# A two-layer hybrid decoder step: the S5 branch computed ahead of the retention's, sampled rows spread over more tiles, and the first tiles behind each norm multiplied before the inverse root is known

## What is computed

```python
u = rmsnorm(h, norm_g);  z = u @ w_in                 # one projection feeds three branches and three gates
s5_out  = glu(gelu(s5_scan(z_s5) + d*z_s5))           # complex diagonal state space, 32 groups of 16 channels
ret_out = silu(g) * groupnorm(retention(q, k, v))     # 4 heads, dk 128, dv 256
conv_out = silu(layernorm(depthwise_conv31(glu(z_conv))))
merged = sig(gate_s5)*(s5_out@s5_proj) + sig(gate_ret)*(ret_out@ret_proj) + sig(gate_conv)*(conv_out@conv_proj)
x = h + merged @ w_out
x = x + ffn(rmsnorm(x))     # layer 0: dense SwiGLU (2816); layer 1: top-2 of 8 experts (3584)
```

## Time and profile before

| | us |
|---|---|
| three runs | 1994.47, 2006.04, 2010.76; median 2006.04 |
| profiled execution | 2003.79 |
| its span (first to last instruction) | 2002.0 |

### The profile page before, as it was taken

One profiled execution on the slowest core, in us unless ns is written; L12 is line 12 of the kernel. 1 busy time (PEld: TensorE's weight loads), 2 busy tenths in 40 slices (PEclk: granted clock), 3 DMA queues, 4 the chain that ended last, 5 costly groups with the idle time before them and its releaser, 6 DMA issues.

```text
span 2002.0 us, 31584 instructions
## 1 busy us (share of the span) xinstructions
PE 1876.1 (94%) x11792; PEld 1591.1 (79%) x11792; DVE 1563.6 (78%) x1767; ACT 1198.4 (60%) x1277; POOL 364.9 (18%) x489
## 2 busy tenths in 40 slices
PE   7977799989998987999999999999999999999995
PEld 6866599979998976899877777777777777777774
DVE  6986697765545966877488888888888988889886
ACT  4343355444444452646476877777777776777775
POOL 7995109940000143000000000000000000000000
PEclk8998899989999997999799999999999999999998
DMA  5546754445555729455589999999999999999996
GB/s 186 171 121 164 148 174 153 165 148 181 179 179 157 212 84 244 110 173 169 220 332 353 382 364 369 373 364 382 355 369 367 373 380 356 370 363 378 381 352 237
DMA packets 98098, 527.54 MB, mean 264 GB/s; under 512 B 11863, under 2 KB 13431, under 8 KB 54359
## 3 DMA queue, kind: packets, MB, share of 16 engines
q1 hardware_dynamic: 86167, 488.69, 66.6%
q0 software_dynamic: 10784, 36.50, 8.0%
q10 hardware_dynamic: 1056, 1.08, 0.2%
HBM read 505.69 MB, written 20.54 MB: 263 GB/s over the span
## 4 chain that ended last, share of the span: by engine, by line
PE 76%; DVE 11%; issue 4%; DMA 4%; ACT 4%; POOL 0%; DVEq 0%; ACTq 0%; SPq 0%; POOLq 0%
PE bank L628 23%; PE bank L630 23%; PE bank L629 23%; DVE ring_parts L1423 2%; DMA out_ret_s<-zone 2%; DVE s5m_parts L1918 2%; DVE zone L1550 1%; PE bank L1000 1%; DMA zone<-in_sret 1%; PE bank L661 1%; ACT zone_parts L1364 1%; PE bank L954 1%; ACT ring_parts L1059 1%; DVE tmp L1614 1%; DVE zone L1446 0%
## 5 line engine op out<-in xcount | busy, mean ns | idle before, releaser
L1918 DVE TENSOR_TENSOR s5m_parts<-s5m,ring_parts 128x2048 fp32r<-128x2048 f32 x228 | 519.2, 2287 | 75.6 <-ACT ring_parts L1364 75.0
L1364 ACT ACTIVATE ring_parts<-s5m 128x2048 fp32r<-128x2048 f32 x228 | 431.7, 1917 | 87.0 <-DMA s5m<-in_experts 80.9
L1423 DVE TENSOR_TENSOR ring_parts<-ring,ring_parts 128x1024 fp32r<-128x1024 f32 x238 | 311.5, 1313 | 203.8 <-ACT ring_parts L1059 177.8
L628 PE MATMUL bank<-uT_parts,ring_parts 128*128 128x264 f32 x1312 | 388.4, 296 | 30.5 <-DVE uT_parts L1440 19.0
L629 PE MATMUL bank<-uT_hi,ring_parts 128*128 128x264 f32 x1312 | 382.4, 291 | 0.0
L630 PE MATMUL bank<-uT_hi,ring_parts 128*128 128x264 f32 x1312 | 381.2, 291 | 0.0
L628 PE MATMUL bank<-s5m_parts,work_parts 128*112 128x512 f32 x896 | 359.3, 401 | 1.1 <-DVE table_parts L1910 1.1
L1059 ACT ACTIVATE ring_parts<-ring 128x1024 fp32r<-128x1024 f32 x238 | 251.2, 1057 | 161.5 <-PE bank L630 125.7
L1918 DVE TENSOR_TENSOR s5m_parts<-s5m,zone_parts 128x2048 fp32r<-128x2048 f32 x112 | 256.0, 2289 | 54.8 <-ACT zone_parts L1364 54.7
L628 PEld LDWEIGHTS bank<-uT_parts,ring_parts 128*128 128x128 f32 x1312 | 257.8, 197 | 39.3 <-issue 35.7
L629 PEld LDWEIGHTS bank<-uT_hi,ring_parts 128*128 128x128 f32 x1312 | 258.5, 197 | 0.1
(11 more groups left out here) (333 smaller groups left out, 2997.9 us busy)
## 6 DMA issues: line engine op xcount, KB each, us to landing
s5m<-in_experts SPq DMA_DIRECT2D x340, 1024.0 KB, 6.6
ring<-in_weights SPq DMA_DIRECT2D x238, 512.0 KB, 3.3
work<-in_sret POOLq DMA_DIRECT2D x8, 512.0 KB, 7.1
zone<-in_sret POOLq DMA_DIRECT2D x8, 512.0 KB, 7.8
out_ret_s<-work POOLq DMA_DIRECT2D x8, 512.0 KB, 9.3
s5m<-kscr POOLq DMA_DIRECT2D x16, 256.0 KB, 13.2
out_ret_s<-zone POOLq DMA_DIRECT2D x8, 512.0 KB, 11.3
xT<-in_xT SPq DMA_DIRECT2D x1, 1056.0 KB, 5.1
```

The lines of the kernel that those rows point to most:

```text
L628: pe.matmul(out, left[0], right[1], start=first, stop=False)
L1364: act.activation(high_slot(c), slot(c, s5m), ACT.Copy).then_inc(high_done, 1)
L1423: dve.tensor_tensor(weights(c, ring_parts), weights(c, ring), f32(weights_hi(c)), ALU.subtract).then_inc(low_done, 1)
L1918: dve.tensor_tensor(slot(c, s5m_parts), slot(c, s5m), f32(high_slot(c)), ALU.subtract).then_inc(low_done, 1)
```

## The change

1. **Order.** The weight stream and `tile_order` put S5's tiles first. `gg0`, `gg1` stand ahead of `win`. Samples 0 to 3 stand at gg1, gg3, gg4 and gg6 (`SAMPLE_BEHIND`), 4 and 5 around `gl`, 6 and 7 within the first `gs`/`ps` pairs. `y`, `gs0`, `yt`, `gs1`, `gl`, `gs`/`ps` come ahead of `gm`, `gr0`, `gv`, `gr1`, `gr`/`pr`. `cm` and `cv` stand behind pr4 and pr5. S5's gated result goes to a buffer of its own (`m5`) and is added when the retention's is merged.
2. **Folded norm.** For `cb`, `ca` of each layer and for `fg`, `fu` 0 to 3, the tile is multiplied with x * weight (parts "x" and "w", `gained`), and the inverse root is put on the result: DVE scales the PSUM tile by rstd. The normed u (or n) is made in the meantime, two parts per tile, for the tiles behind.
3. **DMAs.** `xin` (ten) and `toep` (eight) are issued by SP between the weight chunks, and `kscr` is laid out so that `toep` reads whole rows. `vecs` is loaded ahead of x.
4. **POOL.** The negation of `cli` goes into its factors (two small instructions for eight). Layer 1's build starts at fu1 of layer 0.
5. **Conv steps.** `CONV_AT` is 5 and 4 steps per `gs`/`ps` pair (layers 0 and 1), 6 per `gr`/`pr` pair for the first four, and the rest as listed.

```diff
-CONV_AT = {..., "si": (16, 12), "os": (2, 1), "gr": (6, 6),
-           "gs": (3, 2)}
+CONV_AT = {..., "si": (16, 12), "os": (2, 1), "y": (4, 2),
+           "gs": (5, 4), "gr": (6, 6)}
+SAMPLE_BEHIND = {3: 1, 4: 2, 6: 3}
+FOLDED = 4
 # tile_order
+        add("gg", 2, KD)
         add("win", 8)
         add("kk", 2)
         add("si", 4)
...
+        o += sample(l, 0)
+        for d in range(2, KD):
+            o += [((l, "gg", d), KD)]
+            if d in SAMPLE_BEHIND:
+                o += sample(l, SAMPLE_BEHIND[d])
         add("y", 4)
+        o += [((l, "gs", 0), KD)]
+        add("yt", 4)
+        o += [((l, "gs", 1), KD)] + sample(l, 4)
+        add("gl", 4, 4)
+        o += sample(l, 5)
+        for d in range(KD):
+            if d >= 2:
+                o += [((l, "gs", d), KD)]
+            if d == 2:
+                o += sample(l, 6)
+            o += [((l, "ps", d), 4)]
+            if d == 3:
+                o += sample(l, 7)
...
+        add("gm", 4)
+        o += [((l, "gr", 0), KD)]
+        add("gv", 4)
         o += [((l, "gr", 1), KD)]
 # SP, in the loop over chunks n
+                for l in range(DEPTH):
+                    step = n - RING - CHUNK_OF[(l, "k", 0)]
+                    if step == 0:
+                        sp.wait_ge(zscr_out, 16 * (l + 1))
...
+                    if n == CHUNK_OF[(l, "gg", 3)] + RING:
+                        sp.wait_ge(kscr_out, 16 * (l + 1))
+                        for s in range(S):
...
 # ACT
+            def gained(l, part, col, d):
+                act.activation(parts(part, d)[0], xT[:, d, :], ACT.Copy, scale=vec(l, col, d)).then_inc(x_high, 1)
...
                 for d in range(KD):
                     act.wait_ge(u_ready, 2 * KD * l + d + 1)
                     high((l, "u", d), uT[:, d, :])
+                    if d % 2 == 1:
+                        m = d // 2
+                        evicted_by_dve((l, "cb", m))
+                        act.activation(sigb[:, m, :], sigb[:, m, :], ACT.Sigmoid, bias=vec(l, V_PWB, 4 + m)).then_inc(sig_done, 1)
 # DVE
+            def gained(l, part, col, d):
+                dve.wait_ge(x_high, PART[(l, part, d)])
+                high, to = parts(part, d)
+                dve.scalar_tensor_tensor(out=to, in0=xT[:, d, :], scalar=vec(l, col, d), in1=f32(high),
+                                         op0=ALU.mult, op1=ALU.subtract).then_inc(x_low, 1)
...
+            low_weights(0)
+            for d in range(KD):
+                gained(0, "x", V_GM, d)
+            low_weights(1)
             dve.wait_ge(lam_act, 4)
...
+                inverse_root((l, "ms1", 0), 7 * l + 1)
                 link(dve.memset(xc[:, :, 0:TAPS - 1], 0.0))
                 for m in range(4):
+                    for d in (2 * m, 2 * m + 1):
+                        normed(l, V_GM, d)
+                    key = (l, "cb", m)
+                    full(key)
+                    mul(sigb[:, m, :], at(key)[:, 0:T], rstd[:, 0, :]).then_inc(freed(key), 1)
+                    if m > 0:
+                        for d in (2 * m - 2, 2 * m - 1):
+                            low((l, "u", d), uT[:, d, :])
...
                     for f in range(F_DENSE):
+                        if f < FOLDED:
+                            for d in (2 * f, 2 * f + 1):
+                                normed(l, V_GF, d)
+                            key = (l, "fg", f)
+                            full(key)
+                            mul(gate[:, f % 2, :], at(key)[:, 0:T], rstd[:, 0, :]).then_inc(freed(key), 1)
+                            for d in (2 * f, 2 * f + 1):
+                                low((l, "n", d), uT[:, d, :])
+                            key = (l, "fu", f)
+                            full(key)
+                            link(mul(hT[:, f, :], at(key)[:, 0:T], rstd[:, 0, :]))
+                            dve.wait_ge(gate_on, f + 1)
+                            mul(hT[:, f, :], hT[:, f, :], gate[:, f % 2, :]).then_inc(freed(key), 1)
+                            continue
```

More of the change, by code:

```diff
@@ L112, in tile_order @@
             o += [((l, "pr", d), KD)]
[L113 to L116, removed]
+            if d == 4:
                 add("cm", 1)
@@ L774, in _ @@
                 mm.then_inc(mm_done, 1)
+                for d in range(2):
+                    weight_tile((l, "gg", d), "u", KD)
                 pe.wait_ge(gb_ready, l + 1)
@@ new lines, in _ @@
+                for m in (2, 3):
+                    act.wait_ge(glu_done, 4 * l + m + 1)
+                    high((l, "g", m), glu[:, m, :])
+                masked(7)
+                for d in range(2, KD):
+                    evicted_by_dve((l, "ps", d - 2))
+                    gate_of("gs", d, d % 2)
+                    if d == 5:
+                        key = (l, "os", NS - 1)
+                        copy_out(key, os_rows, at(key)[:, 0:DV])
+                    if d == 7:
+                        key = (l, "ot", 0)
+                        full(key)
+                        for half in range(2):
+                            last = act.activation(vT[:, half:KD:2, SEQ:T],
+                                                  at(key)[:, half * P:(half + 1) * P].rearrange("p (h x) -> p h x", h=HEADS)[:, :, 0:NS],
+                                                  ACT.Copy)
+                        last.then_inc(freed(key), 1)
@@ new lines, in _ @@
+                for h in range(HEADS):
+                    evicted_by_dve((l, "gm", h))
+                    if h >= 2:
+                        full((l, "gv", h - 2))
+                    c = (h % 2) * 2 * T
+                    act.activation(sq[:, c:c + 2 * T].rearrange("p (x t) -> p x t", x=2), vT[:, 2 * h:2 * h + 2, :],
+                                   ACT.Square).then_inc(squares, 1)
+                    if h == 1:
+                        evicted_by_dve((l, "ps", KD - 2))
+                        gate_of("gr", 0, 0)
+                    if h >= 1:
+                        root((l, "gv", h - 1), 1.0 / DV)
@@ L1245, in _ @@
+                root((l, "gv", 3), 1.0 / DV)
+                for m in range(KD):
+                    if m == 4:
+                        evicted_by_dve((l, "ps", KD - 1))
+                        gate_of("gr", 1, 1)
+                    act.wait_ge(gated, KD * l + m + 1)
+                    high((l, "r", m), vT[:, m, :])
                 for d in range(2, KD):
@@ L1323, in _ @@
                         x_square(d)
+                        gained(l + 1, "x", V_GM, d)
             l = DEPTH - 1
@@ L1520, in phases, with inverse_root @@
                 mul(W(1), W(14), W(14)).then_inc(phase_ready, 1)
-            def normed(key, gains, turn, part):
+            def inverse_root(key, turn):
                 low_weights(CHUNK_OF[key] + 2)
@@ L1527, in normed @@
                 dve.wait_ge(*out_of(key))
-                for d in range(KD + 2):
-                    if d < KD:
-                        dve.scalar_tensor_tensor(out=uT[:, d, :], in0=xT[:, d, :], scalar=gains(d), in1=rstd[:, 0, :],
-                                                 op0=ALU.mult, op1=ALU.mult).then_inc(u_ready, 1)
-                    if part and d >= 2:
-                        low((key[0], part, d - 2), uT[:, d - 2, :])
+            def normed(l, col, d):
+                dve.scalar_tensor_tensor(out=uT[:, d, :], in0=xT[:, d, :], scalar=vec(l, col, d), in1=rstd[:, 0, :],
+                                         op0=ALU.mult, op1=ALU.mult).then_inc(u_ready, 1)
             conv_at = [0, 0]
```

479 lines of the change are left out of this document (252 added, 227 removed).

## The result

| kernel | median us | runs |
|---|---|---|
| before | 2002.5 | 20 (1994.5 to 2010.8) |
| after | 2009.9 | 20 (19 within 2004.1 to 2013.8, one at 4840.3) |

The ratio is 1.004, with a 95% interval of 1.003 to 1.005; the one execution of 4840.3 counts as slow and is left out of it. The forecast was 1981, a clear gain. The profiled execution after took 2008.0 (span 2006.2), against 2003.8 and 2002.0. The change moved a great deal and earned nothing. Part 1 of the page after stands against the earlier trace rows: PE is 9.5 us less busy, and the span is 4 us longer.

What follows compares the result with a forecast made beforehand. TensorE, busy 94% of the span, was taken as the bound: its work plus its holes. The terms -16.9 - 7.1 - 8.8 + 4 + 6 + 0 gave -22.8 from 2003.8, so 1981 us, range 1946 to 2012.

Steps and rivals of the forecast that it cites:

- A: Layer 0's mixer, samples spread and S5 moved forward: 45.1 us removed, 28.2 added, so -16.9 (bounds -33 and 0).
- B: The same reorder in layer 1's mixer: -7.1 us (bounds -20 and +6).
- (1) and (2): Added up to y: s0 uncovered behind si, 2.9 us; DVE's work exceeding PE's, 4.3, and 1.0 more in layer 0.
- (4): Retention norm's serial DVE chain, gm to pr0's end: 28.2 us against PE's 15.7, a new wait of 12.5.
- C: Conv norm earlier, covered by gr7, pr7, gc0 and gc1: -8.8 us in both layers (bounds -9 and -2).
- D: Folded tiles at layer 1's front: weight splits form a ring, zs2 at 41.4 against 37.5, +4 us (bounds -7 and +12).
- E: Layer 0's front, same ring of weight splits: zs2 at 60 against 53.9, +6 us (bounds -7 and +12).
- F: Feed-forward's fold: -2.9 us from the fold, +2.9 from POOL's build beside it, 0 in sum (bounds -12 and +11).
- R1: Rival: the fold works, weight chunks split in time in all three places; 1945 us, chance 0.18.
- R2: Rival: the fold costs clock, falling to 1.2 GHz in the rings; +27, 2008 us, chance 0.14.
- R4: Rival: half clock also from gg2 to y and behind the retention's wait, granted clock 0.7; 2036 us, chance 0.12.
- R3: Rival: state transfers hidden in neither order, sample steps 4 to 7 wait as before; 2008 us, chance 0.06.

Runs made afterwards that it cites:

- e7: Kernel after, with only the two stores of small pieces (out_conv_s, out_h_s) held until gm is done: 1984.2 us, 0.992 of before.
- e1: Kernel after, with GpSimd's five result stores held until gm is done on TensorE, both layers: 1982.6 us, 0.992 of before.
- e8: e1 with the kernel matrix's store to kscr and the issue of toep moved earlier: 1979.4 us, 0.991 of before.
- e11: Kernel before the change, with GpSimd's five result stores held until pr0 is done (254 in place of 219 to 224): 2017.8 us, 1.007 of before.
- e6: e1 with the fold at the head of both layers taken back (cb and ca on the normed u): 1974.0 us, 0.987 of before.
- e5_ffn: e1 with the fold ahead of the feed-forward taken back (fg and fu on the normed n): 1983.5 us, 0.993 of before.
- e12: e9 with gm one S5 pair earlier, gv ahead of gr0, and gr0's gate behind the four roots: 1969.7 us, 0.984 of before.
- e9: Kernel after with stores held, kernel matrix's store and toep early, and both folds taken back: 1969.6 us, 0.983 of before.

## Why the prediction was wrong

**The step that failed** is in A and B, and it is one assumption made twice: that transfers are free when their own consumer is far away. For the weights it was "I cost this at nothing", argued by when gs1 would be wanted. For toep it was argued for the chunks behind it and not for y, its own consumer. And POOL's stores are in no sum: the moved order was followed on SP's queue, and not past the point to which the sample steps moved GpSimd's program. They cost 25.7 to 27.3 in the median (e7, e1). toep's lateness shows as 14.0 of waits before y. e8 takes all but 1.8 of them and is 3.2 under e1, so most of that wait hid other lateness. The stores are shown as the cause, by taking them out (e1, e7) and by putting them in the old order (e11).

**A.** Forecast -16.9, found +2.4. With the stores held and toep early (e8) the same stretch is 204.4, that is -16.9; with the stores alone (e1) it is -12.9. So the working of A was near for what it counted: the states no longer hold a sampled output, xin is in time, s0 waits 2.89 (forecast 2.9). Terms (1) and (2) were 8.2 up to y, and e8 has waits of 2.9, 2.5, 2.1 and 2.6 there. That e8 meets -16.9 to the tenth is chance, as it also issues toep earlier than the forecast's kernel did. **The retention norm's chain** (4) was 28.2 in the forecast. In e1 it is 27.6 from ps7's end to pr0's, and in the kernel after 39.5, with the 9.5 before gm and its half clock in it. But the one wait of some 12 at pr0 that was to show it is three, within pr0 (2.5, 2.2 and 2.3 in e1); the rest is a wait of 1.0 before gv and half clock (0.79 from 261.8 to 289.6 of e1).

**B.** Forecast -7.1, found +3.0; e1 has -7.9 and e8 -8.1.

**C.** Forecast -8.8 in both layers, found -6.3. gc1 was forecast without a wait and waits 1.74 for a weight split; the clock from gc7 to wo7 of layer 0 is 1.00, where it was 0.94. Layer 1 was forecast at -1.8 and is +2.0; no run asks why.

**D and E.** The ring was right in kind and in layer 0 nearly in size: cb2 starts at 24.7 (forecast 25.3), zs2 at 62.0 (60). In layer 1 the waits before cb2, cb3, ca0 and ca1 are 1.44, 0.68, 1.34 and 1.36, where 1.5 to 2.5 were forecast, so D was +1.4, not +4. I had not asked what each head would be with all else of the change in place and the fold left out. That is 9.6 us better at v7 in layer 0 (e6), not 6, and no different in layer 1.

**F.** Forecast 0, found -4.1: the fold +1.1, and 5.2 the other way, which the traces put to the build's later start. I had charged the moved build to the pairs it falls on and forgot to credit the norm that it leaves. The charge of +2.9 was not seen either: from 427 to 449 of the kernel after, with POOL busy 19.2 of 21.9 us, a split takes 1.31 (forecast 1.51) and a normed step 0.52 (forecast 0.86). POOL's steps beside those normed ones are of 16 to 128 columns; those of the earlier trace rows fell on the build's wide steps. The size that the norm lost before is 810 against 492 ns for a normed step. The Trainium skill (SBUF — State Buffer, "Who interferes with whom") has a VectorE instruction with two SBUF inputs contend with a GpSimd instruction that reads SBUF, and these rows agree in sign. By the rule at its worst F would have been +12; nothing of that size was seen.

**The rivals.** R1 (the fold works): no, weight splits were late, by 1.1 to 1.3 in each pair of the feed-forward. R2 and R4 (clock): no; two of the three rings ran at 1.00 in spite of their holes, and layer 0's head at 0.92, near the 0.91 of before. From gg2 to gg7 the clock was 0.85 (165 to 193.7), not R4's 0.7. R3 (state transfers hidden in neither order): no sampled output waits for a state. It had the right resource and the wrong victim: the transfers hurt the weights and toep. None of them named the cause.

Of the store in small pieces, the Trainium skill (DMA: Bandwidth & Descriptors, "Specifications") says that transfers under 512 B fall off the full rate; the 28 to 61 GB/s with the engines busy agree. The Trainium skill (DMA: Bandwidth & Descriptors, "Queues, rings and completion order") has each transfer engine take turns between the queues, packet by packet; by that rule any store on another queue slows the weights for as long as it lasts. No run here shows the turns themselves. The size is not in the rule: beside out_ret_p a chunk took 3.8 us, beside out_conv_s 12.1.

## What to carry to other kernels

When a step moves, list where every transfer behind it in that engine's program now falls, and ask which loads it meets; count the transfers by the time they hold the engines (480 KB in 120 B pieces held them some 20 us), not by bytes. An engine that splits operands ahead in program order turns a late load into a late anything: the wait was charged to a copy that had nothing to do with weights. And a change made of several parts should be tried part by part: here a store's place was worth 27 us and one fold cost 9. The reorder looked like a loss, and with the stores held and toep early its two stretches (A and B) are 25.0 shorter than before, by e8's trace; no run took the reorder alone.

## What the runs showed that was not expected

- A 480 KB store in 120 B pieces took 20.1 us beside the weights and 15.0 in e7, where it met few of them. About the same volume in long rows (out_ret_p, 512 KB) took 7.8 in e7.
- Much the same holes came with two clocks. From wo7 to fu4 the kernel after has waits of 2.1 and then 1.1 to 1.3, and ran at 1.00. e1 has 2.1 and then 1.1 to 1.3 as well, one fewer, and ran at 0.96, with half clock in its first tile; e5_ffn, with one wait of 4.7, had 0.95. Around pr0 one wait or three made little difference: up to its end the mean is 0.65 with one of 9.7 (263 to 277.8 of e12) and 0.68 with three of 2.5, 2.9 and 2.3 (263.7 to 277.1 of e9). What sets it is open.

```profile
395.00:433.40 38.40, 32.77 (x244) 31.28 (x244) 27.58 (x43) 20.04 (x32) 18.97 (x38) 0.96 0.50 154
...
397.10:434.60 37.50, 32.23 (x246) 31.14 (x246) 22.34 (x33) 19.63 (x30) 14.72 (x34) 0.95 0.50 158
```

(Busy time by stretch, e1_stores and e5_ffn.)

- DVE's normed steps took 810 ns beside POOL's steps of 288 columns (before), and 492 with POOL idle (e5_ffn): 1.65 times. Beside POOL's narrow steps (after, 427 to 449) they took 518.
